# Half of the second expert pair's down matrices loaded into the region of the normed input and its squares

## The reference

```
g_idx    = argmax over 4 groups of  h @ w_rg + b_rg
top_v,_  = the 2 largest of the chosen group's 8 expert logits
gate     = softmax(groups)[g_idx] * softmax(top_v)
for each of 32 experts e and the tokens routed to it:
    hid = silu(xb @ w_gate[e]) * (xb @ w_up[e])      # 1024 -> 512
    y   = hid @ w_down[e]                            # 512 -> 1024
    out[token] += gate * y
```

## Time and profile before

| what | value |
|---|---|
| median of three runs | 1966.14 us |
| the profiled execution | 1962.46 us |
| its span, first to last instruction | 1960.6 us |
| granted TensorE clock, mean | 0.994 |
| PE busy in the span | 1923.6 us (98%) |
| bytes moved by DMA | 591.75 MB |
| experts of the first expert layer | about 894 to 1359 us |
| experts of the second expert layer | about 1485 to 1950 us |

### The profile page before, as it was taken

One profiled execution on the slowest core, in us unless ns is written; L12 is line 12 of the kernel. 1 busy time (PEld: TensorE's weight loads), 2 busy tenths in 40 slices (PEclk: granted clock), 3 DMA queues, 4 the chain that ended last, 5 costly groups with the idle time before them and its releaser, 6 DMA issues.

```text
span 1960.6 us, 24533 instructions
## 1 busy us (share of the span) xinstructions
PE 1923.6 (98%) x10178; PEld 1290.6 (66%) x10178; DVE 584.7 (30%) x1353; ACT 419.4 (21%) x936; POOL 12.5 (1%) x27
## 2 busy tenths in 40 slices
PE   8999999999999999999999999999999999999998
PEld 7798888857988887675544554555885544544544
DVE  3279540432755504422111111112222111111111
ACT  3440000322301012423112212212013212112212
POOL 1000000000001000000000000000000000000000
PEclk9999999999999999999999999999999999999999
DMA  9747674522467841227999999999337999999995
GB/s 308 247 172 281 276 311 183 225 86 92 167 279 300 334 180 44 87 86 312 425 433 433 429 433 433 430 435 425 140 127 290 424 430 436 430 433 433 429 434 222
DMA packets 39274, 591.75 MB, mean 302 GB/s; under 512 B 5010, under 2 KB 13466, under 8 KB 15138
## 3 DMA queue, kind: packets, MB, share of 16 engines
q1 hardware_dynamic: 38626, 588.63, 72.9%
q10 hardware_dynamic: 576, 2.10, 0.3%
HBM read 585.24 MB, written 1.05 MB: 299 GB/s over the span
## 4 chain that ended last, share of the span: by engine, by line
PE 74%; DMA 23%; DVE 2%; ACT 1%; issue 0%; DVEq 0%; SPq 0%
PE ps L465 27%; DMA ring<-in_w_up 22%; PE ps L1128 16%; PE ps L706 8%; PE ps L1225 4%; PE ps L1110 2%; PE ps L1116 2%; PE ps L753 2%; PE ps L535 2%; PE ps L624 1%; PE ps L553 1%; PE ps L567 1%; PE ps L909 1%; PE ps L1261 1%; PE ps L952 1%; PE ps L520 1%
## 5 line engine op out<-in xcount | busy, mean ns | idle before, releaser
L1128 PE MATMUL ps<-ring,work 128*64 128x512 f32 x2048 | 450.0, 593 | 6.6 <-DMA ring<-in_w_up 6.4
L465 PE MATMUL ps<-h,ring 128*128 128x256 f32 x2064 | 452.6, 381 | 3.0 <-DVE h L2067 2.2
L465 PEld LDWEIGHTS ps<-h,ring 128*128 128x128 f32 x2064 | 392.4, 191 | 62.0 <-issue 9.3
L1128 PEld LDWEIGHTS ps<-ring,work 128*64 128x64 f32 x2048 | 149.4, 137 | 299.2 <-issue 287.6
L1444 ACT ACTIVATE work<-ps 128x512 f32<-128x512 f32 (+1 forms) x184 | 94.4, 519 | 738.8 <-PE ps L465 333.6
L1225 PE MATMUL ps<-ring,work 128*64 128x512 f32 x1024 | 226.8, 595 | 1.6 <-DVE work L2267 1.6
L1444 ACT ACTIVATE work<-ps,ada,scale_g 128x128 f32<-128x128 f32 x256 | 96.2, 456 | 389.0 <-PE ps L1110 389.0
L2258 DVE TENSOR_TENSOR work<-ps,work 128x512 f32<-128x512 f32 x30 | 20.8, 692 | 518.5 <-ACT work L1444 518.5
L1225 PEld LDWEIGHTS ps<-ring,work 128*64 128x64 f32 x1024 | 70.6, 137 | 133.7 <-issue 128.0
L706 PE MATMUL ps<-work,ring 128*128 128x256 f32 (+1 forms) x704 | 148.6, 373 | 0.0
L1790 DVE SCALAR_TENSOR_TENSOR work<-ring,silu_c,work 128x512 f32<-128x512 f32 x196 | 143.8, 754 | 5.1
(11 more groups left out here) (298 smaller groups left out, 1195.1 us busy)
## 6 DMA issues: line engine op xcount, KB each, us to landing
ring<-in_w_up SPq DMA_DIRECT2D x32, 4096.0 KB, 21.9
ring<-in_w_down SPq DMA_DIRECT2D x32, 4096.0 KB, 16.7
ring<-in_w_gate SPq DMA_DIRECT2D x30, 4096.0 KB, 19.4
ring<-in_w_ada SPq DMA_DIRECT2D x24, 2048.0 KB, 8.6
ring<-in_w_ff_gate SPq DMA_DIRECT2D x10, 2048.0 KB, 13.6
ring<-in_w_ff_up SPq DMA_DIRECT2D x10, 2048.0 KB, 14.1
ring<-in_w_ff_down SPq DMA_DIRECT2D x8, 2048.0 KB, 13.6
ring<-in_ml_w_in SPq DMA_DIRECT2D x6, 2048.0 KB, 10.1
```

The lines of the kernel that those rows point to most:

```text
L465: last = mm(ps[:, b, 0:T], w[:, k, m * P:(m + 1) * P], rhs[:, k, :], start=(k == 0), stop=(k == nk - 1))
L1128: last = mm(ps[e * CAP:(e + 1) * CAP, j, :], xg[:, k, e * CAP:(e + 1) * CAP], w[e][:, k, :], start=(k == 0), stop=(k == last_k), skip_grou ...
```

## The change

`h` and `sq` become the two halves of one buffer `h_sq`, and the same bytes get a third view, `early_rows`: for each of two experts 16 KB in all, 8 KB per expert and partition. In the gathered path SP now issues, before anything else and without a wait, a 2 MB load of the first half (two of four row blocks, k = 0 and 1) of both down matrices of pair 1 into `early_rows`. The load of D(1) into the ring, which still waits for `down_done` of pair 0, carries only the second half, 2 MB. On PE pair 1 is taken out of the loop and written out, so that its `down` can read k = 0 and 1 from `early_rows` (after the new semaphore `early_down`) and k = 2 and 3 from the ring. The loop now covers pairs 2 to 14. Two more semaphores per layer were needed, so four others were merged into two: `f_ln` and `gate_expm` into `gate_logs`, `z_gelu` into `z_stats`; each is counted in the same order as before.

```diff
-        h = sb("h", [P, KT, T])
-        sq = sb("sq", [P, KT, T])
+        h_sq = sb("h_sq", [P, 2, KT, T])
+        h, sq = h_sq[:, 0], h_sq[:, 1]
+        early_rows = h_sq[:].rearrange("p e k t -> p e (k t)")
...
-                def down(i):
+                def down(i, early=False):
                     pe.wait_ge(e_["hg_ready"], i + 1)
-                    pe.wait_ge(arrived[2], 16 * i + loads[2])
+                    if early:
+                        pe.wait_ge(e_["early_down"], 16)
+                    else:
+                        pe.wait_ge(arrived[2], 16 * i + loads[2])
                     for c in range(2):
                         for k in range(HTL):
+                            if early and c == 0 and k == HTL // 2:
+                                pe.wait_ge(arrived[2], 16 * i + loads[2])
                             for e in range(2):
                                 at = k * PAIR + e * CAP
+                                wd = pair_of[e][2][2][:, k, :]
+                                if early and k < HTL // 2:
+                                    wd = early_rows[:, e, k * D:(k + 1) * D]
                                 last = mm(ps[e * CAP:(e + 1) * CAP, c, :], hg[:, at:at + CAP],
-                                          pair_of[e][2][2][:, k, c * 512:(c + 1) * 512],
+                                          wd[:, c * 512:(c + 1) * 512],
                                           start=(k == 0), stop=(k == HTL - 1))
...
-                with pe.Fori(0, last_pair - 1) as n:
-                    gate_and_up(n + 1, 2 * n + 1)
+                def whole_pair(i, yt_before, early=False):
+                    gate_and_up(i, yt_before)
                     turn_weights()
                     scatter()
-                    turn_hidden(n + 1)
-                    gather_next(n + 1)
-                    down(n + 1)
+                    turn_hidden(i)
+                    gather_next(i)
+                    down(i, early)
+
+                whole_pair(1, 1, early=True)
+                with pe.Fori(0, last_pair - 2) as n:
+                    whole_pair(n + 2, 2 * n + 3)
...
                 def pairs_of_gathered_tokens():
 
                     freed = e_["gate_full"], e_["up_full"], e_["down_done"]
+                    down_1 = weights[2][l, 1].rearrange("p (e c) -> p e c", e=2)
+                    sp.dma_start(early_rows, down_1[:, :, 0:SLOT // 2]).then_inc(e_["early_down"], 16)
...
-                    for w in (1, 2):
-                        sp.wait_ge(freed[w], 1)
-                        load_pair(w, 1)
+                    sp.wait_ge(freed[1], 1)
+                    load_pair(1, 1)
+                    sp.wait_ge(freed[2], 1)
+                    arrived, slots = slots_of(2)
+                    sp.dma_start(slots[:, :, SLOT // 2:SLOT], down_1[:, :, SLOT // 2:SLOT]).then_inc(arrived, 16)
```

More of the change, by code:

```diff
@@ L314, in build @@
                  "ln_centred ln_normed ln_sigmoid mixed proj_copied ffn_sig ffn_gate_read hidden mq mo mv "
-                 "gates_tok gates_head gate_args f_ln gate_a row_max gate_expm acol_ready exponents decays weighted "
-                 "den_read head_out sums_read y_ready f_sum f_root f_ready att_copied u_gelu z_gelu z_centred z_stats z_normed "
+                 "gates_tok gates_head gate_args gate_logs gate_a row_max acol_ready exponents decays weighted "
+                 "den_read head_out sums_read y_ready f_sum f_root f_ready att_copied u_gelu z_centred z_stats z_normed "
                  "k_rope_read q_rope_read rotated maxima exps turned_dve turned_act sink_ready sink_exp norms_ready norm_rows att_normed logits_read "
@@ L321, in build @@
         layer_names = ("diag row_full row_copied gate_full gate_sig gate_freed up_full up_freed hid_ready "
-                       "down_done masks_ready gate_half all_root weights_turned spread_ready gathered xg_ready gated half_done hid_turned hg_ready yt_ready scattered").split()
+                       "down_done early_down masks_ready gate_half all_root weights_turned spread_ready gathered xg_ready gated half_done hid_turned hg_ready yt_ready scattered").split()
         E = [{n: sem(f"expert_{n}_{l}") for n in layer_names} for l in range(2)]
@@ L909, in _ @@
                     last = mm(ps[:, b, :], h[:, k, t * P:(t + 1) * P], w[:, k, :], start=(k == 0), stop=(k == KT - 1))
-                close_bank(b, last, tiles_act, S["z_gelu"])
+                close_bank(b, last, tiles_act, S["z_stats"])
             release(n, tiles_act)
@@ L1618, in _ @@
             turn.own(achain)
-            turn.give(A(ghead[:, 2, :], ghead[:, 2, :], ACT.Ln, bias=1.0), S["f_ln"])
+            turn.give(A(ghead[:, 2, :], ghead[:, 2, :], ACT.Ln, bias=1.0), S["gate_logs"])
             turn.take(S["gate_args"])
-            turn.give(A(ghead[:, 3, :], ghead[:, 3, :], ACT.Exp, scale=-1.0), S["gate_expm"])
+            turn.give(A(ghead[:, 3, :], ghead[:, 3, :], ACT.Exp, scale=-1.0), S["gate_logs"])
             for n in range(HEADS):
@@ L1649, in _ @@
             for t in range(TT):
-                turn.give(A(z_a[:, t, :], tile(), ACT.Gelu), S["z_gelu"])
+                turn.give(A(z_a[:, t, :], tile(), ACT.Gelu), S["z_stats"])
             def att_exp(i):
@@ L2005, in _ @@
             step(stt(ghead[:, 2, :], ghead[:, 1, :], -1.0, ghead[:, 1, :], ALU.mult, ALU.max), S["gate_args"])
-            turn.take(S["f_ln"])
+            turn.take(S["gate_logs"])
             step(stt(ghead[:, 1, :], ghead[:, 1, :], 0.0, ghead[:, 2, :], ALU.min, ALU.subtract))
@@ L2040, in _ @@
             turn.take(S["den_read"])
-            turn.take(S["gate_expm"])
+            turn.take(S["gate_logs"])
             step(V.tensor_tensor(ghead[:, 0, :], ghead[:, 0, :], ghead[:, 3, :], ALU.max))
@@ L2093, in z_centre @@
             def z_centre(t):
-                turn.take(S["z_gelu"])
+                turn.take(S["z_stats"])
                 step(V.tensor_reduce(small[:, 0:1], z_a[:, t, :], AX, ALU.add))
```

## The result

The changed kernel takes 1972.05 us (median of 8 runs, 1970.63 to 1975.02); the kernel before, run beside it, takes 1965.26 us (8 runs, 1962.3 to 1967.37). The ratio is 1.0035, with a 95% interval of 1.0025 to 1.0044: slower by about 6.8 us. The forecast was 1964.8 us and a range of 1961.5 to 1968. It was wrong, in its sign too. What came is one of its own rivals, "the branch", which had been given a chance of 0.10 and a time of 1970.1 us.

What follows compares the result with a forecast made beforehand. PE sets the pace early in each expert layer, the DMA's load stream later, once its lead is used up. Stream gain -3.5, packets +1.6 and branch +0.6 sum to -1.3 us on 1966.14: 1964.8 us, range 1961.5 to 1968.

Steps and rivals of the forecast that it cites:

- the branch: Rival, PE's branch into the gathered path: each waits for the early load, 3 us a layer, 1970.1 us; chance 0.10.
- The branch: the step that failed: PE's branch before the experts: the early load lengthens it by 0.3 us a layer, 0.6 in all; bounds 0 to 3.
- each longer branch shows: PE's branch beside the first half gate product: 3.3 and 3.4 us, its cover used up, so any lengthening adds in full.
- The stream's gain: Weight loads after the smaller D(1): of 4.85 us a layer, 1.8 and 1.7 remain at D(2); 3.5 for both layers.
- G(2), for which I used 12.5: Gate load of pair 2: 12.5 us from issue on a nearly idle DMA, landing at 943.4, 4.0 us earlier.
- The packet: Pair 2, from the written-out pair: at least one more instruction packet among the loads, 0.8 us a layer, 1.6 in all.
- from D(3) on there is no gap: Load stream from pair 3's down load on: issued before the load ahead has landed, so no further gain is lost.
- The first wait for an up load: Sign, PE's up products: first wait later than pair 6 by a layer's net gain over 0.53; 1.8 us means three pairs.
- a branch above 4.5 us: Sign of a wrong prediction: PE's branch before the experts exceeds 4.5 us instead of staying near 3.4.
- The full credit: Rival, load stream: it keeps all 4.85 us a layer, 9.7 in all, giving 1956.4 us; chance 0.12.
- the gain without the two costs: Rival: gap-limited gain of 3.5 to 4.3 us, packet and branch costing nothing, 1961.8 to 1962.6 us; chance 0.15.
- The change does nothing to the stream: Rival: early load meets G(1), or U(2)'s instruction packet keeps an engine behind; D(2) lands no sooner, 1967.7 us; chance 0.13.

Runs made afterwards that it cites:

- e1: Changed kernel with the early load issued behind the first half of G(1), after PE's branch; 1968.95 us, ratio 1.0017 to the kernel before.
- e5: Changed kernel with PE's two paths exchanged, so the gathered path follows directly and the jump comes at its end; 1968.72 us, ratio 1.0005 to the kernel before.
- e2: Changed kernel with the early load issued but unused, D(1) loaded whole, pair 1 back in the loop; 1971.22 us, ratio 1.0031 to the kernel before.
- e7: Changed kernel with an early load of 1 MB, issued behind the first half of G(1), and D(1) of 3 MB; 1966.23 us, ratio 0.9997 to the kernel before.
- e4: Changed kernel with an early load of 1 MB in the same place and D(1) of 3 MB; 1967.44 us, ratio 1.0004 to the kernel before.
- e3: Changed kernel without the early load: pair 1 still written out, D(1) loaded whole into the ring; 1968.37 us, ratio 1.0011 to the kernel before.
- e10: Changed kernel with the early load issued about 1.9 us later, when pair 0's masks are done; 1972.39 us, ratio 1.0028 to the kernel before.
- e9: Kernel before with early load, written-out pair and PE's gathered path directly behind the branch in the second layer only; 1966.1 us, ratio 0.9999.

## Why the prediction was wrong, point by point

**The branch: the step that failed.** It was valued at 0.3 us a layer, "near the first, because the packet of rows 8 got through in a saturated stretch within its 2.5 us window". It measured 2.7 and 2.4 us (gaps), the branch itself 2.7 and 2.5 longer. The window of the earlier trace rows showed that a packet moved, not when it had been asked for, so it said nothing on how long it had waited. The packets of straight stretches (at 965 and 1337 us, say) came with no gap of PE beside them, however long they may have been on their way; at the taken branch PE's next instructions came only with its end, 2.4 us behind the packet. The other half of the step was right: the cover was used up, and "each longer branch shows". e1 takes the load away from the branch, e5 the branch away from the load, and either removes the gap; e2 has the gap alone, 5.4 us of the loss. The Trainium skill ("Runtime: NRT & Kernel Launch", Instruction fetch mechanics) says that a taken branch outside the window of instructions held must have its target's page brought by DMA first. The prediction cited it and sided against it; the one packet of 16 KB in each branch, with the end always 2.3 to 2.8 us behind it, and the missing packet at the untaken branch of e5 agree with it. Nothing here shows by what the packet was held up. With the rival's 3 us in place of 0.3 the prediction's own sum was +4.0, 1970.1.

**The stream's gain: mis-sized.** I took 1.8 and 1.7 us, measured 0.8 (14.5 to 13.7) and 0.9 (14.4 to 13.5). The mechanism was right: D(2) stays tied to PE's pace, its issue comes 28.58 us behind D(1)'s (929.40 to 957.98) as before, and 4.85 us shrink in the gaps. D(2) was issued 2.45 us before U(2) had landed (960.43) and still landed 11.25 us behind it, not 9.7. Two things are in this number. One is the restart: in all the traces a 4 MB load that met no packet landed 9.7 us behind the one ahead (at most 10.0) if it had been issued over 5 us before that one landed, and 9.7 to 10.3 us behind it at 4.3 to 5. The other is the packet that I had counted by itself, as the next paragraph shows: D(2) met it. In e5, where D(2) met none, it took 12.5 and 13.3 us:

```profile
ring<-in_w_down SPq DMA_DIRECT2D x1, 4096.0 KB, 12.5
```

That is 2.0 and 1.1 us of gain, near my 1.8 and 1.7. The parts can't be told apart, for loads without a packet on an emptying DMA differ as much (12.1 to 13.9). G(2), for which I used 12.5, took 12.5 in the second layer and 14.3 in the first, where it met a packet at 944.0.

**The packet: one where I had put it, and a dear one elsewhere.** I took 1.6 for both layers. One packet came at 966.2 us, and in the second layer at 1565.1, while D(2) was under way. The window 957 to 972 us:

```profile
q8 instruction: 1, 0.02, 0.4%
```

D(3) landed 10.1 and 10.0 us behind U(3) instead of 9.7, but met no packet: it is the restart again, for it was issued 4.5 and 4.35 us before U(3) had landed; so "from D(3) on there is no gap" was wrong by 0.4 and 0.3 us. Gain, this packet and D(3) together leave 0.4 and 0.6 us a layer, where the prediction had 1.0 and 0.9. The dear packet was one that I hadn't foreseen, near the end of the first layer. The window 1336 to 1338.5 us, and the load that it met (issued 1319.3):

```profile
q8 instruction: 1, 0.02, 2.8%
...
ring<-in_w_up SPq DMA_DIRECT2D x1, 4096.0 KB, 23.4
```

23.4 instead of 21.9: this is the wait of 1.9 us, 1.5 above the others. A longer program moved the place at which the next instructions are fetched: before, that packet came at 1339.8 us, behind the load's landing (1314.14 + 21.88 = 1336.0), and met D(15), which PE wasn't waiting for. All the kernels with the pair written out in the first layer and its branch at the start have the packet inside U(15), and it cost 1.5 us (e7), 1.3 (e4), 0.7 (e3, e10) and 0.2 (e1, with the changed kernel's own PE program). What sets its cost stays open.

**The sum.** First layer: 2.7 - 0.8 + 0.4 + 1.5 = +3.8 (measured +3.9). Second: 2.4 - 0.9 + 0.3 = +1.8 (measured +2.0). Together +5.6 against 5.9 in the stages and 6.8 in the medians, whose interval is 4.9 to 8.7. The prediction had +0.6 for the branches, and they took 5.1; that alone turns its -1.3 into a loss. U(15)'s 1.5 us stood in no term.

**The signs that were named.** The first wait for an up load was to come later by the net gain over 0.53. It came one pair later (waiting from 1086.16, where the pattern of the earlier trace rows begins at 1051.92): a net gain of some 0.5 us. The sign for a wrong prediction, a branch above 4.5 us, came true. One reading was off without harm: the earlier trace rows have nine slices at 425 to 436 GB/s in the first expert layer and seven in the second, not eight in each.

**The rivals.** The full credit is refuted by D(2)'s landing; the gain without the two costs by the branch. "The change does nothing to the stream" is near the truth for the stream alone, with 0.4 and 0.6 us, but has no branch in it. Its idea that U(2)'s own packet keeps D(2) late wasn't tested. Whether the change without its branch would gain at all isn't settled: e5 and e9 can't be told from the kernel before (ratios 1.0005 and 0.9999), and no version tried beat it.

## What to carry to other kernels

Before a load is put into an idle stretch of the DMA, look for a taken branch there (here PE's), and at how far its cover reaches: here the idle DMA was what let the branch end in time. A packet seen in a busy window doesn't show that it was cheap; measure from the asking to the arrival. And a megabyte taken from a stream that is tied to an engine's pace gives only what is left after the next gap, 0.8 to 2.0 of 4.85 us here, so look for the next issue that doesn't move before counting it. Before two runs are compared to 1 us, compare their granted clocks.

## What was not expected of the hardware

- A taken branch of PE to the far path took 3.3 to 3.8 us with the DMA idle (seven kernels) and 5.7 to 6.5 us with loads under way, in seven kernels and at two places of the program. Its packet of 16 KB starts 0.9 to 1.05 us after it in the first case, 3.3 to 4.2 in the second; 2.3 to 2.8 us remain behind it in both. The size of the load's runs (4, 8, 16 KB) hardly changes it. The branch at the end of each turn of the loop took 0.2 us, and q8 moved no packet from 966.2 to 1337.1 us while the loop ran.
- One instruction packet met by U(15) cost that load 0.2 (e1), 0.7 (e3, e10), 1.3 (e4) and 1.5 us (the changed kernel, e7). By what these differ is open.
- A 4 MB load on an idle or emptying DMA took 12.1 to 13.9 us without a packet in it, up to 15.1 with one (e10) and once 16.3 (e9), where one in a full stream lands 9.7 us behind the one ahead. Issued over 5 us before the one ahead had landed, it lost 0 to 0.3 us; at 4.3 to 5 us, up to 0.6.
- The part ahead of the experts ended at 894.2 and at 899.1 us in two executions of one kernel, 4.9 us apart: more than this change's gain could ever have been. The granted clock ahead of it accounts for 5.0.
